# Two transformer blocks on one core: modulation by row products on VectorE in place of products and column sums on TensorE

## The chip, the core and the metric

The kernel runs on one core of one Trainium2 chip. Its metric is the device time of one execution in microseconds. Engines are named as the profile names them: PE is TensorE (PEld its weight loads), DVE is VectorE, ACT is ScalarE, POOL is GpSimd, SP is SyncE; a trailing q is the engine's own queue, from which it also issues DMAs. SBUF is the on-chip memory of 128 partitions, PSUM the accumulators that PE writes (banks `PB0` to `PB7`).

## The reference, cut to what matters

Two residual blocks over 256 tokens of width 1024, f32. Each block is modulated by a condition vector `c`: a vector-matrix product gives six vectors of 1024, which shift, scale and gate the two halves of the block.

```python
mod = jnp.einsum('bd,de->be', c, w_mod[l]) + b_mod[l]          # block 2: silu(c_2) @ w_ada_2 + b_ada_2
sh1, sc1, gt1, sh2, sc2, gt2 = jnp.split(mod, N_MOD, axis=-1)  # 6 x 1024
h = modulate(rmsnorm(x, norm1_g[l]), sh1, sc1)                 # norm * (1 + sc1) + sh1
z = jnp.einsum('bsd,de->bse', h, w_in[l])
...                                                            # pool mixer and attention, gated: y
x = x + gt1[:, None, :] * jnp.einsum('bsd,de->bse', y, w_out[l])
h2 = modulate(rmsnorm(x, norm2_g[l]), sh2, sc2)
x = x + gt2[:, None, :] * peer_ffn(h2, ...)                    # 16384 experts, rows of u and v
```

The weight matrix of the modulation is 1024 x 6144 f32 in each block, 24 MB. Block 2 has the same frame with other attention.

## The kernel before, in words

The kernel is five programs, one for each engine, ordered by semaphores that are written out by hand. Three of them share one long list of 651 weight tiles of 128 x 1024 f32 (512 KB). `SP` loads tile after tile into a ring of four slots. For each tile ACT rounds it to its high part (`WH`, line 1182, `fill` of the ACT program), DVE subtracts to get the low part (`WL`, line 1639, `fill` of the DVE program), and PE multiplies three products of high and low parts (lines 477 to 479, helper `three`). `WH` and `WL` hold three tiles (`NW`), so ACT may start tile t when PE has used tile t - 3 (`s_used`). `fill(k)` in a program means: see that tiles up to k + 2 are done; all other work of ACT and DVE stands between the `fill` calls, in program order.

Order of block 1: first norm and the modulation that it needs (chunks 0 to 7); pool input tiles, forget tile `W_F`; four Q steps and four K steps of two tiles each; the mixing loop `for i in range(10)`, two tiles a turn, which computes V and the output gates and beside them the attention of two heads a turn; then output projection, second norm, expert queries, the U phase (128 tiles of expert rows, activations), and the V phase (128 tiles, sums into four PSUM banks). Block 2 follows.

In a turn i of the mixing loop, PE runs `scores(i)` (lines 683, 686), `values(i - 2)` (711), one tile, `weights(i - 1)` (transposes, 698), one tile, and a step of the modulation. DVE runs `fill`, divides the exponentials of turn i - 1 by their sums (1819 to 1821), adds the mask to the scores of turn i and takes their maximum (1831, 1834), `fill`, copies of V (i < 4) and of y (i >= 2; line 1643), and, for i = 6 and 8, `mixed` for two parts of y (1805 to 1808); after i = 8 the diagonals for the broadcast of the gate (1729). ACT runs `fill`, the exponentials (1346), `fill`, copies of the turned weights (1186), sigmoids of the gates (1327; i = 5, 7, 9) and the modulation's step.

The modulation is cut into 48 chunks of 256 outputs, 24 a block, 1024 KB each. In block 1 (`mod_chunk`, line 544) PE multiplies the condition, padded to 32 columns, with a chunk, four partial sums on 32 partitions apart; ACT copies the result to `MR` (`chunk_out`), and `columns` (line 523) multiplies with ones, two one-column matmuls that put 2 x 128 outputs on partitions in `PB0`; DVE adds the bias (1649). Chunks 8 to 11 stand in the Q and K steps, 12 to 19 in turns 0 to 7, 20 to 23 after the output projection. `mod_step(g)` is the columns of the chunk before and the products of chunk g. ACT loads chunk g + 2 behind `chunk_out(g)` into two buffers. In block 2's modulation (chunks 24 to 47, in the V phase of block 1) DVE makes the partial sums instead (`chunk_step`: eight multiplications or multiply-adds by a value on each partition, 128 x 256, lines 2014 and 2017, two for each V tile); PE does the `columns` of chunks 24 to 35 in the V phase, and those of 36 to 47 (`LATE`) between the blocks, before `transposed(2)` (line 558), which waits for DVE's scaled rows (1646). The square of X at the start is DVE's line 1734.

## Time and profile before

| | us |
|---|---|
| median of 3 runs (2184.76 to 2185.3) | 2185.13 |
| the profiled execution: span from first to last instruction | 2183.5 |
| PE busy in it | 2135.9 |
| DVE busy | 1591.9 |
| ACT busy | 1297.9 |

The profile is that of one execution. In a timeline, a line is a run of equal instructions: start, us that they took, engine, line of the kernel, operation, output<-inputs, and in square brackets how long the engine had been idle before and what ended that. Matmuls overlap each other, so their distances are read between starts. In the groups the numbers after the bar are busy us, mean ns of one, and idle time before.

### The profile page before, as it was taken

How to read it: one execution, taken by the hardware profiler on the slowest of the kernel's cores; microseconds unless marked ns; L12 is line 12 of the kernel's file. 1: busy time of each engine (PE TensorE's matmuls, PEld its weight loads, DVE VectorE, ACT ScalarE, POOL GpSimd, SP SyncE). 2: the span in 40 equal slices, each digit the busy share in tenths (PEclk: the TensorE clock that was granted, in tenths of full speed). 3: DMA queues.
4: the chain of work that ended last, by engine and by line, in shares of the span. 5: the costliest groups of instructions: out<-in, count | busy, mean ns of one | idle time of the engine just before them, and what ended most of it. 6: DMA issues, size and time to landing. Idle time of an engine off the chain costs nothing.

```text
span 2183.5 us, 36554 instructions
## 1 busy us (share of the span) xinstructions
PE 2135.9 (98%) x13700; PEld 1904.0 (87%) x13700; DVE 1591.9 (73%) x3503; ACT 1297.9 (59%) x2442; POOL 100.4 (5%) x136
## 2 busy tenths in 40 slices
PE   7999999999999999999999998999999999999998
PEld 5988888888999988888889988888899998888886
DVE  3455659898888767888866655798988887555556
ACT  3355545666999754445545544565679986555554
POOL 0000000303000000000000000013030000000000
PEclk9999999999999999999989999999999999999999
DMA  8665566665444467778744634666654445566664
GB/s 334 203 210 180 178 184 185 200 185 183 136 127 127 155 202 284 282 276 289 257 145 135 204 97 129 187 189 194 192 172 127 126 127 174 182 194 193 194 194 133
DMA packets 110495, 407.42 MB, mean 187 GB/s; under 512 B 11504, under 2 KB 11888, under 8 KB 110064
## 3 DMA queue, kind: packets, MB, share of 16 engines
q1 hardware_dynamic: 98880, 361.81, 53.1%
q10 hardware_dynamic: 11440, 43.28, 5.1%
q8 instruction: 110, 1.80, 0.4%
q14 instruction: 65, 0.53, 0.1%
HBM read 403.99 MB, written 1.05 MB: 185 GB/s over the span
## 4 chain that ended last, share of the span: by engine, by line
PE 93%; DVE 3%; ACT 2%; issue 1%; POOL 1%; DMA 0%; ACTq 0%; DVEq 0%
PE PB L477 20%; PE PB L479 20%; PE PB L478 20%; PE PB L889 11%; PE PB L887 6%; PE PB L861 6%; PE PB L812 2%; PE PB L886 2%; PE PB L544 1%; PE PB L811 1%; PE PB L828 1%; PE PB L558 1%; PE PB L523 1%; POOL AR L2346 1%; DMA X<-in_x 0%
## 5 line engine op out<-in xcount | busy, mean ns | idle before, releaser
L1639 DVE TENSOR_TENSOR WL<-RING,WH 128x1024 fp32r<-128x1024 f32 x651 | 801.9, 1233 | 444.2 <-ACT WH L1182 442.1
L1182 ACT ACTIVATE WH<-RING 128x1024 fp32r<-128x1024 f32 x651 | 686.7, 1055 | 438.7 <-PE PB L479 430.9
L477 PE MATMUL PB<-WH,HX 128*128 128x512 f32 (+2 forms) x1344 | 494.4, 368 | 7.2 <-DVE HX L1694 3.3
L479 PE MATMUL PB<-WH,HX 128*128 128x512 f32 (+2 forms) x1344 | 490.5, 365 | 0.0
L478 PE MATMUL PB<-WL,HX 128*128 128x512 f32 (+2 forms) x1344 | 490.1, 365 | 0.0
L477 PE MATMUL PB<-HX,WH 128*128 128x256 f32 x1440 | 424.6, 295 | 6.8 <-DVE HX L1694 6.0
L479 PE MATMUL PB<-HX,WL 128*128 128x256 f32 x1440 | 409.4, 284 | 0.0
L478 PE MATMUL PB<-HX,WH 128*128 128x256 f32 x1440 | 409.1, 284 | 0.0
L889 PE MATMUL PB<-HX,WH 128*128 128x512 f32 x1092 | 389.1, 396 | 0.0
L887 PE MATMUL PB<-HX,WL 128*128 128x256 f32 x1248 | 322.4, 279 | 0.0
L477 PEld LDWEIGHTS PB<-WH,HX 128*128 128x128 f32 x1344 | 255.3, 190 | 51.4 <-issue 4.9
L479 PEld LDWEIGHTS PB<-WH,HX 128*128 128x128 f32 x1344 | 255.4, 190 | 40.4
L478 PEld LDWEIGHTS PB<-WL,HX 128*128 128x128 f32 x1344 | 255.5, 190 | 39.3
L477 PEld LDWEIGHTS PB<-HX,WH 128*128 128x128 f32 x1440 | 278.1, 193 | 13.2 <-issue 10.1
L478 PEld LDWEIGHTS PB<-HX,WH 128*128 128x128 f32 x1440 | 277.8, 193 | 0.3
L479 PEld LDWEIGHTS PB<-HX,WL 128*128 128x128 f32 x1440 | 277.1, 192 | 0.0
L887 PEld LDWEIGHTS PB<-HX,WL 128*128 128x128 f32 x1248 | 235.2, 188 | 13.5
L889 PEld LDWEIGHTS PB<-HX,WH 128*128 128x128 f32 x1092 | 204.9, 188 | 42.1
L1186 ACT ACTIVATE AR<-PB 128x256 f32<-128x256 f32 (+2 forms) x237 | 96.7, 415 | 220.3 <-PE PB L889 131.0
L1433 ACT ACTIVATE OH<-KC,GIT 128x128 f32<-128x128 f32 x512 | 162.4, 392 | 3.3 <-DVE GIT L1998 3.3
L2044 DVE TENSOR_SCALAR OH<-KC,GIT 128x128 f32<-128x128 f32 x512 | 142.3, 344 | 0.1
L861 PE MATMUL PB<-OH 128*128 128x128 f32 x1024 | 137.6, 277 | 1.9
(239 smaller groups left out, 2075.7 us busy)
## 6 DMA issues: line engine op xcount, KB each, us to landing
RING<-in_u SPq DMA_DIRECT2D x256, 512.0 KB, 3.7
RING<-in_v SPq DMA_DIRECT2D x256, 512.0 KB, 4.2
RING<-in_win SPq DMA_DIRECT2D x90, 512.0 KB, 3.9
AR<-in_wm ACTq DMA_DIRECT2D x40, 1024.0 KB, 6.5
RING<-in_wq SPq DMA_DIRECT2D x32, 512.0 KB, 3.7
AR<-in_wm SPq DMA_DIRECT2D x8, 1024.0 KB, 16.3
RING<-in_wout SPq DMA_DIRECT2D x16, 512.0 KB, 3.6
RING<-in_sk SPq DMA_DIRECT2D x8, 512.0 KB, 3.6
```

The lines of the kernel that those rows point to most:

```text
L477: e.matmul(o, ah, bh, start=start, stop=False)
L478: e.matmul(o, ah, bl, start=False, stop=False)
L479: return e.matmul(o, al, bh, start=False, stop=stop)
L812: r = e.matmul(PB[b][:, :], wh[:, k, :], HX[:, k, :], start=k == 0, stop=k == KT - 1)
L861: r = e.matmul(PB[b][:, 128 * t:128 * t + 128], OH[:, i, 0, t, :], OH[:, i, 1, t, :], start=True, stop=True)
L887: r = e.matmul(PB[b][:, 0:256], wl[:, m, :], HH[:, m, :], start=False, stop=False)
L889: r = e.matmul(PB[b][:, :], wh[:, m, :], HX[:, m, :], start=False, stop=m == KT - 1)
L1182: e.activation(hi(t), raw(("w", t), words(t)), ACT.Copy).then_inc(s_hi, 1)
L1186: e.activation(dst, src, ACT.Copy).then_inc(done, 1)
L1433: n = own.mark(e.activation(OH[:, i, 0, t, :], iota, ACT.Abs, scale=-1.0, bias=GIT[:, 1, 4 * q + t:4 * q + t + 1]))
L1639: e.tensor_tensor(lo(t), raw(("w", t), words(t)), hi(t).bitcast(F32), ALU.subtract).then_inc(s_lo, 1)
L2044: r = e.tensor_scalar(OH[:, i, 1, t, :], iota, GIT[:, 2, c:c + 1], GIT[:, 0, c:c + 1], ALU.is_equal, ALU.mult)
```

## The change

Chunks 8 to 19 of block 1 (the mixing gate and the second norm's shift and scale) and all 24 of block 2 are computed on DVE alone. Their weights are stored transposed, 128 outputs on partitions and the 1024 inputs along the row (`wr1`, `wr2`), and a chunk is two such halves. The condition is loaded as the same row on all partitions (`cr1`, `cr2`, 512 KB each, into the unused one-hot buffers `OH`). One `tensor_tensor_reduce` (`row_sum`) multiplies a half with the condition, in place, and writes its sum into the column of `MC` where the output belongs; the bias is added there (`add_rows`). PE and ACT have no part in these chunks but for their loads, which ACT issues (`rows_in`), into three buffers in block 1 and two in block 2, behind a wait for DVE's count `s_mr` or `s_mdv`. In the Q steps DVE makes 0, 1, 2, 2 row products, in each K step 2, in turn 0 of the mixing loop 2, and in turns 1 to 9 one. In the V phase it makes one behind every second tile. The Silu of block 2's condition moves from the start (8 columns) to the V phase (`n == 12`, 1024 columns). Chunks 0 to 7 and 20 to 23 stay as they are.

```diff
+MODS = [0, 4, 1, 5, 2, 6, 3, 7] + list(range(8, 24))
 N_START = 8
+N_ROWS = 12
+ROW_SLOT = {N_START + i: i % 3 if i < 11 else 0 for i in range(N_ROWS)}
+ROW_SLOT.update({24 + i: i % 2 for i in range(24)})
+ROW_LAND = {g: sum(ROW_SLOT[h] == s for h in ROW_SLOT if h <= g) for g, s in ROW_SLOT.items()}
...
-        PLACES = [ar(o, n, 2, 4, 256) for o, n in ((26112, 2), (1024, 4), (1024, 2))]
+        GATE2 = ar(1024, 4, 2, 4, 256)
+        ROWS1, ROWS2 = ar(26112, 3, 2, D), ar(1024, 2, 2, D)
         MR0 = ar(19232, N_START, 256)
-        LATE = 36
-        MRV = ar(8192, 48 - LATE, 256)
         COND = OH[:, 0, 0, 0:2, :].rearrange("p a (b n) -> p (a b) n", b=4)
+        CR = [OH[:, i, :, :, :].rearrange("p a t n -> p (a t n)") for i in (1, 0)]
...
+                    e.dma_start(CR[0], cr1).then_inc(s_cr, 16)
...
+                    e.wait_ge(s_gp, 64)
+                    e.dma_start(CR[1], cr2).then_inc(s_cr, 16)
...
-            def mod_step(g):
-                if g not in (N_START, 12):
-                    columns(g - 1)
-                mod_chunk(g)
...
-            mod_step(8)
...
-                    mod_step(9)
...
-            mod_step(10)
...
-                    mod_step(11)
...
-            columns(11)
...
-                if i < 8:
-                    mod_step(12 + i)
                 if i == 8:
-                    columns(19)
...
                     r.then_inc(s_used, 1)
-                    if blk == 0 and IN_V.get(n - 5, LATE) < LATE:
-                        columns(IN_V[n - 5])
...
-            for g in range(LATE, 48):
-                columns(g)
...
+            def rows_in(g, done=0):
+                if done:
+                    e.wait_ge(s_mr, done)
+                e.dma_start(row_chunk(g), row_source(g)).then_inc(chunk_landed(g)[0], 16)
...
-            e.activation(SM[:, C_C2:C_C2 + 8], SM[:, C_C2:C_C2 + 8], ACT.Silu).then_inc(s_silu, 1)
...
-                    chunk_in(8)
-                    chunk_in(9)
+                    for g in range(N_START, N_START + 3):
+                        rows_in(g)
...
+                if c == 3:
+                    rows_in(11, 1)
...
+                rows_in(12 + c, 2 + c)
...
+                if i < 3:
+                    rows_in(16 + i, 6 + i)
+                if i == 6:
+                    rows_in(19, 10)
...
+                    if blk == 0 and n == 12:
+                        e.wait_ge(s_cr, 32)
+                        e.activation(CR[1], CR[1], ACT.Silu).then_inc(s_silu, 1)
...
+            def add_rows(c0, c1, b_col, n):
+
+                e.tensor_tensor(MC[:, c0:c1], MC[:, c0:c1], SM[:, b_col:b_col + c1 - c0], ALU.add).then_inc(s_mod, n)
+
+            def row_sum(g, j):
+
+                w, c = row_chunk(g)[:, j, :], 2 * g + j
+                if j == 0:
+                    e.wait_ge(*chunk_landed(g))
+                if (g, j) == (N_START, 0):
+                    e.wait_ge(s_cr, 16)
+                if (g, j) == (24, 0):
+                    e.wait_ge(s_silu, 1)
+                r = e.tensor_tensor_reduce(w, w, CR[g // 24], 1.0, 0.0, ALU.mult, ALU.add, MC[:, c:c + 1])
+                if j:
+                    r.then_inc(s_mr if g < 24 else s_mdv, 1)
+
+            row_next = [0]
+
+            def row_sums(n):
+                for _ in range(n):
+                    row_sum(N_START + row_next[0] // 2, row_next[0] % 2)
+                    row_next[0] += 1
...
                 fill(k + 1)
+                row_sums((0, 1, 2, 2)[c])
...
                 fill(W_K + 2 * c + 1)
+                row_sums(2)
+                if c == 2:
+                    e.wait_ge(s_mr, 4)
+                    add_rows(16, 24, C_B1 + 16, 1)
...
-                if i == 0:
-                    e.wait_ge(s_mcol, 12)
-                    add_bias(0, C_B1, 16, 24)
+                row_sums(2 if i == 0 else 1)
...
-                    e.wait_ge(s_mcol, 20)
-                    add_bias(0, C_B1, 24, 40)
+                    e.wait_ge(s_mr, N_ROWS)
+                    add_rows(24, 40, C_B1 + 24, 1)
...
+            def chunk_step(n):
+
+                n0, t = n - (n - V_FIRST) % 4, (n - V_FIRST) % 4
+                if n0 in IN_V and t % 2:
+                    row_sum(IN_V[n0], t // 2)
...
-                        if IN_V.get(n - 7) == LATE - 1:
-                            e.wait_ge(s_mcol, LATE)
-                            add_bias(48, C_B2, 0, 24)
+                        chunk_step(n)
+                        if IN_V.get(n - 4) == 47:
+                            e.wait_ge(s_mdv, 24)
+                            add_rows(48, 96, C_B2, 2)
...
+    def rows(w):
+        n = w.shape[1] // 256
+        return w.reshape(1024, n, 2, 128).transpose(1, 3, 2, 0)
```

## Rows read from the trace of the kernel before

**Rows 1.** The page, part 1: busy us of each engine, share, instructions.

```profile
PE 2135.9 (98%) x13700; PEld 1904.0 (87%) x13700; DVE 1591.9 (73%) x3503; ACT 1297.9 (59%) x2442; POOL 100.4 (5%) x136
```

**Rows 2.** Groups by line and form: count, busy us, mean ns, idle before.

```profile
L544 PE MATMUL PB<-AR,OH 128*32 128x256 f32 x384 | 29.1, 431 | 9.6 <-DMA AR<-in_wm 9.4 <-DVE MC L1649 0.2
...
L523 PE MATMUL PB<-KC,MR 128*128 128x1 f32 x112 | 14.0, 229 | 0.0
...
L523 PE MATMUL PB<-KC,AR 128*128 128x1 f32 x80 | 11.1, 263 | 1.1 <-ACT AR L1186 1.1
```

**Rows 3.** Timeline of PE in the mixing loop: start us, us, engine, line, operation.

```profile
134.32 0.50 PE L523 MATMUL PB<-KC,MR 128*128 128x1 f32 x4
134.76 1.07 PE L544 MATMUL PB<-AR,OH 128*32 128x256 f32 x16
135.76 0.49 PE L683 MATMUL PB<-AR 64*128 64x128 f32 x4
...
141.04 0.82 PE L698 MATMUL PB<-KC,AR 128*128 128x128 f32 x6
...
144.56 0.50 PE L523 MATMUL PB<-KC,MR 128*128 128x1 f32 x4
```

**Rows 4.** The same, chunk 8.

```profile
55.78 1.94 PE L544 MATMUL PB<-AR,OH 128*32 128x256 f32 x16
```

**Rows 5.** Timeline of PE and of ACT where K ends.

```profile
116.68 0.50 PE L523 MATMUL PB<-KC,MR 128*128 128x1 f32 x4
117.58 0.49 PE L683 MATMUL PB<-AR 64*128 64x128 f32 x4 [0.40 <-issue]
...
116.88 0.60 ACT L1186 ACTIVATE AR<-PB 128x512 f32<-128x512 f32 x1 [1.76 <-PE PB L479]
```

**Rows 6.** Timeline of DVE at the start: the square of X.

```profile
11.46 1.23 DVE L1734 CUSTOM_DVE_ANT_0 AR<-X 128x1024 f32<-128x1024 f32 x1 [5.71 <-DMA X<-in_x]
12.61 0.08 DVE L1734 DVE_READ_ACCUMULATOR2_ANT ST<- 128x1 f32 x1
```

**Rows 7.** Timeline of DVE in two iterations of the mixing loop.

```profile
178.71 1.23 DVE L1639 TENSOR_TENSOR WL<-RING,WH 128x1024 fp32r<-128x1024 f32 x1 [2.81 <-ACT WH L1182]
...
180.91 0.35 DVE L1821 TENSOR_SCALAR AR<-AR 128x256 f32<-128x256 f32 x1
...
184.89 1.23 DVE L1639 TENSOR_TENSOR WL<-RING,WH 128x1024 fp32r<-128x1024 f32 x1 [2.08 <-ACT WH L1182]
...
186.37 0.42 DVE L1805 TENSOR_TENSOR AR<-AR 128x256 f32<-128x256 f32 x1
...
188.63 1.22 DVE L1639 TENSOR_TENSOR WL<-RING,WH 128x1024 fp32r<-128x1024 f32 x1
```

**Rows 8.** Timeline of ACT in the same stretch.

```profile
183.82 1.04 ACT L1182 ACTIVATE WH<-RING 128x1024 fp32r<-128x1024 f32 x1
```

**Rows 9.** Timeline of PE where the gate is broadcast.

```profile
205.02 0.50 PE L523 MATMUL PB<-KC,MR 128*128 128x1 f32 x4
206.43 0.35 PE L567 MATMUL PB<-AR,KC 128*128 128x128 f32 x1 [0.91 <-DVE AR L1729]
```

**Rows 10.** Timeline of PE in the V phase, around one column sum.

```profile
823.63 0.50 PE L523 MATMUL PB<-KC,MR 128*128 128x1 f32 x4
...
824.31 0.39 PE L478 MATMUL PB<-WL,HX 128*128 128x512 f32 x1
```

**Rows 11.** V phase, busy us (x instructions): PE, PEld, DVE, ACT, POOL; clock, DMA.

```profile
824.00:960.00 136.00, 136.00 (x623) 113.03 (x622) 109.57 (x188) 65.54 (x97) 0.00 (x0) 1.00 0.78 278
```

**Rows 12.** Timeline of PE between the blocks.

```profile
1101.67 5.62 PE L523 MATMUL PB<-KC,AR 128*128 128x1 f32 x48
1108.13 1.12 PE L558 MATMUL PB<-KC,AR 128*128 128x128 f32 x4 [0.84 <-DVE AR L1646]
```

**Rows 13.** The page, part 6: loads of the modulation weights, issue to landing.

```profile
AR<-in_wm ACTq DMA_DIRECT2D x40, 1024.0 KB, 6.5
...
AR<-in_wm SPq DMA_DIRECT2D x8, 1024.0 KB, 16.3
```

More of the change, by code:

```diff
@@ L49 @@
 N_TILES = 651
-MODS = [(0, m) for m in (0, 4, 1, 5, 2, 6, 3, 7)] + [(0, m) for m in range(8, 24)] + [(1, m) for m in range(24)]
+MODS = [0, 4, 1, 5, 2, 6, 3, 7] + list(range(8, 24))
 N_START = 8
+N_ROWS = 12
+ROW_SLOT = {N_START + i: i % 3 if i < 11 else 0 for i in range(N_ROWS)}
+ROW_SLOT.update({24 + i: i % 2 for i in range(24)})
+ROW_LAND = {g: sum(ROW_SLOT[h] == s for h in ROW_SLOT if h <= g) for g, s in ROW_SLOT.items()}
 V_FIRST = 22
@@ L401, in chunk, with row_chunk, nth @@
         def chunk(g):
-            if g < N_START:
-                return START[:, g, :, :, :]
-            return PLACES[0 if g < 20 else 1 if g < 24 else 2][:, g % 4 if 20 <= g < 24 else g % 2, :, :, :]
+            return START[:, g, :, :, :] if g < N_START else GATE2[:, g - 20, :, :, :]
+        def row_chunk(g):
+            return (ROWS1 if g < 24 else ROWS2)[:, ROW_SLOT[g], :, :]
+        def nth(g):
+            return g if g < N_START else g - N_ROWS
         def chunk_landed(g):
@@ L508, in columns @@
             def columns(g):
-                m = MODS[g][1]
+                m = MODS[g]
                 rows = chunk_sums(g)[2]
-                if g < 24:
-                    e.wait_ge(s_mev, g + 1)
-                else:
-                    e.wait_ge(s_mdv, g - 23)
-                if g in (24, LATE):
-                    e.wait_ge(s_mod, 7 if g == 24 else 8)
-                if g < N_START and g > 1:
-                    e.wait_ge(s_mod, g // 2)
-                if g in (20, 22):
-                    e.wait_ge(s_mod, 6)
+                e.wait_ge(s_mev, nth(g) + 1)
+                if g > 1:
+                    e.wait_ge(s_mod, min(g // 2, 4))
                 for j in range(2):
@@ L535, in mod_chunk @@
                 else:
-                    e.wait_ge(s_mev, g - 1 if 21 <= g < 24 else g)
+                    if g >= 22:
+                        e.wait_ge(s_mev, nth(g) - 1)
                     if g == 20:
                         e.wait_ge(s_up, 3)
-                    if g in (8, 12):
-                        e.wait_ge(s_mod, {8: 4, 12: 5}[g])
                 e.wait_ge(s_cond, 1)
@@ L1998, in chosen @@
                     e.tensor_copy(GIT[:, s, :], PB[4 + s][:, 0:256]).then_inc(s_git, 1)
-            chunk_sum = [0]
-            def chunk_step(n, half):
-                n0, t = n - (n - V_FIRST) % 4, 2 * ((n - V_FIRST) % 4) + half
-                if n0 not in IN_V:
-                    return
-                g = IN_V[n0]
-                w, rows, c = chunk(g)[:, t // 4, t % 4, :], chunk_sums(g)[2], SM[:, C_C2 + t:C_C2 + t + 1]
-                if t == 0:
-                    e.wait_ge(s_silu, 1)
-                    if g < LATE:
-                        e.wait_ge(s_mcol, g - 1)
-                    e.wait_ge(*chunk_landed(g))
-                    chunk_sum[0] = own.mark(e.tensor_scalar(rows, w, c, None, ALU.mult))
-                    return
-                own.done(chunk_sum[0])
-                r = e.scalar_tensor_tensor(out=rows, in0=w, scalar=c, in1=rows, op0=ALU.mult, op1=ALU.add)
-                if t < 7:
-                    chunk_sum[0] = own.mark(r)
-                else:
-                    r.then_inc(s_mdv, 1)
+            def chunk_step(n):
+                n0, t = n - (n - V_FIRST) % 4, (n - V_FIRST) % 4
+                if n0 in IN_V and t % 2:
+                    row_sum(IN_V[n0], t // 2)
             def peer(blk, n_q, n_u, n_v, gate):
@@ L2326, in peer @@
                             e.wait_ge(s_rope, 6)
+                        else:
+                            e.wait_ge(s_mr, 9)
                         for i in range(16):
@@ L2449 @@
         "u1": experts(i["peer_u"]), "v1": i["peer_v"][0],
-        "wm2": halves(i["w_ada_2"][0]),
+        "wr2": rows(i["w_ada_2"][0]),
         "win2": np.concatenate([tiles(w2[:, :1024]), halves(w2[:, 1024:1536]), tiles(w2[:, 1536:3072]),
```

67 lines of the change are left out of this document (27 added, 40 removed).

## The prediction, made before the changed kernel ran

> **What bounds the kernel now.** I read the page's busy table first, then the groups of instructions, then the timeline of each engine. TensorE (PE) is busy 98% of the span [rows 1]; what shortens the kernel is PE time, and what lengthens it is PE waiting. The modulation costs PE two kinds of work [rows 2]: 384 weight-vector products (16 records for each of 24 chunks) and 192 one-column sums (4 records for each of 48 chunks). The change takes away 12 chunks of the first and 36 of the second. "Busy" overstates them, because matmuls are pipelined; I take distances between starts. In the mixing loop the columns of a chunk take 134.76 - 134.32 = 0.44 us and the products of a chunk 135.76 - 134.76 = 1.00 us [rows 3].
>
> **Part 1, ahead of the mixing loop (chunks 8 to 11).** Four products and four column sums leave PE. Chunk 8 runs at half clock, 1.94 us busy [rows 4] against 1.07 at full clock [rows 3]; the projections that move into this place run at half clock too, so I count it at its full-clock 1.00. Chunks 9, 10, 11: 3.00. Columns 8, 9, 10: 3 x 0.44 = 1.32. Columns 11: nothing. PE starts them at 116.68 and its next work, the first scores, at 117.58, 0.90 later, of which 0.44 is the columns; the scores wait for ScalarE's copy of kT, which runs from 116.88 to about 117.5 whatever PE does [rows 5]. Sum: 5.3 us.
>
> What is put in their place is 13 row products on VectorE (DVE) up to the end of K's four steps, two a step at most. One row product multiplies 128x1024 f32 with 128x1024 f32 and sums it. The nearest row is the square of X at the start, the same instruction with the same sizes: 1.23 us, and its accumulator is read 12.61 - 11.46 = 1.15 after its start [rows 6]. I take 1.17 a product. Two of them are 2.3 us of DVE in front of the next weight tile's subtraction. A tile is let go by PE three tiles ahead of its use, so two tiles of about 2.9 us (3.52 between 141.04 and 144.56 with six transposes in it [rows 3]) lie between; ScalarE takes 1.04 and DVE 1.23 of them [rows 7, 8], which leaves 3.5 us. The products fit, so I cost them at nothing here; this cover is thin in the K step that also scales yaT (3.4 us in the same queue), hence up to 3 us lost at the upper end.
>
> **Part 2, the mixing loop (chunks 12 to 19).** Eight products and eight column sums leave PE: 8 x 1.00 + 8 x 0.44 = 11.5 us. Here I don't believe the whole of it, because a second loop runs beside PE's. An iteration of PE lasts 144.56 - 134.32 = 10.24 us [rows 3], and without the chunk 8.80. The other loop goes DVE low part of a tile, DVE softmax, ScalarE exponentials (in order ahead of its next tile), DVE low part of the second tile, DVE copy of y. From one start, 178.71, to the end of that copy, 186.37, it is 7.66 us [rows 7]; the second tile comes from ScalarE at 183.82, which in its program stands behind the exponentials of this same turn, and DVE sits idle 2.08 us for it [rows 7, 8]. With a row product behind it the loop is 7.66 + 1.17 = 8.83, and 9.16 in iterations 2 and 3, which copy v too (one more copy of 0.33). So the two loops are now equally long, and DVE loses the time in which it used to stand idle.
>
> How far may DVE lag? PE's transposes of the second head come, after the change, 141.04 - 134.32 - 1.44 + 0.28 = 5.56 us behind the boundary of an iteration; DVE has that head ready 180.91 + 0.35 - 178.71 = 2.55 after the low part starts. A lag of more than about 2.95 us stalls PE. I walk through it, lag of the low part's start and then the stall. Iteration 1: 2.45 (two products in iteration 0, no values yet, limit 2.1), 0.3. Iteration 2: 2.95, 0. 3: 3.3, 0.4. 4: 3.3, 0.4. 5: 3.0, 0. 6: 3.3 (ScalarE's sigmoids with a table load come first), 0.4. 7: iteration 6 has `mixed` twice, 188.63 - 186.37 = 2.26 us [rows 7], which was hidden in DVE's idle time: lag 5.3, stall 2.4. Iteration 8 has no scores, so PE comes 1.5 earlier to the transposes and found DVE late already; the chunk's 1.44 taken from it is worth 0.1. Its end is the broadcast of the gate, for which DVE must do copy, row product and `mixed` twice first: PE waited there already (1.41 us from the columns at 205.02 to the broadcast at 206.43, [rows 9]), and by my walk the row product comes on top of that path; these two places give back 2.3. Given back in all: 0.3 + 0.4 + 0.4 + 0.4 + 2.4 + 2.3 = 6.2. Kept: 11.5 - 6.2 = 5.3, say 5.4 because PE had small waits of its own before. The two ends: 0 (every chunk's place taken by a DVE wait) and 11.5.
>
> **Part 3, the V phase of block 1.** Twelve column sums leave PE (chunks 24 to 35). A matmul of this phase follows the one before at 0.23; from the columns' start 823.63 to the second matmul behind them 824.31 it is 0.68 [rows 10], so one column sum costs 0.68 - 0.23 = 0.45 with the pipeline's restart: 12 x 0.45 = 5.4 us, all on the path, as PE is busy 136.00 us of 136.00 there and DVE 109.57 [rows 11]. DVE's eight multiply-adds of a chunk become two row products, 2.3 us in 11.4. One of them lies behind every second tile, less than the 3.5 us of cover. ScalarE gets a `Silu` over the 1024 columns of the second condition with its table load, about 2.4 us once (a 1024-wide tile takes it 1.04 [rows 8]); it has 65.54 busy of 136 [rows 11], so nothing. SyncE's queue gets one more 512 KB load behind the one of `final_g`, whose waits it shares; its extra wait (all gates multiplied) is met before the phase starts. Nothing.
>
> **Part 4, between the blocks.** The last 12 column sums, 48 records, stand at 1101.67; PE then waits for the scaled rows of DVE and starts transposing at 1108.13, "idle before <-DVE L1646" [rows 12]. They fill a wait that DVE's chain sets, and removing them brings nothing. DVE's add of the bias that waited for them goes too (under 0.2 us, behind the broadcast). At the start, ScalarE's Silu goes from a time in which it waits for X, and the first condition's 512 KB load lies behind weights that are used late: nothing.
>
> **Transfers.** Chunks are 1024 KB each as before, and are issued by ScalarE, which now waits for DVE's count in front of an issue; tiles and softmax are queued behind that wait. In my walk the count is there one step before each issue. The three-buffer ring starts with three loads instead of two.
>
> **Sum.** 5.3 + 5.4 + 5.4 = 16.1 us. The profiled span is 2183.5, so the changed one would be 2167.4; the median of the runs, 2185.13, lies 1.6 above that span, so 2169.0 us. The clock adds noise: the stretch at half clock at 55.78 costs 0.9 us in that chunk alone [rows 3, 4], and such stretches can move when the work moves; I allow 2 us either way.
>
> **Rivals.**
> (a) PE keeps everything. If ScalarE's and DVE's loop is shorter than I think, or my lag limits are too strict, it is 5.3 + 0.4 + 11.5 + 5.4 = 22.6: 2162.5 us. For it: DVE is idle 2.08 us in such an iteration [rows 7]. Against it: that idle time is a wait for ScalarE inside the loop, not a reserve. Chance 0.20.
> (b) DVE also delays the Q and K steps. Two products ahead of a tile, the yaT scaling behind them, and chunks that land late: a loss of up to 3 us there, and as much again in the loop if its lag starts larger. Saved about 10: 2175 us. Chance 0.13.
> (c) A row product costs twice my price, 2.3 us. Then a turn of the loop is 7.66 + 2.3 = 10.0. The walk gives turns of 10.5, 9.9, 10.2, 10.2, 9.9, 9.9, 12.3 and 13.1 to the broadcast, 86.0; before it is 81.5 (72.1 from 134.32 to 206.43, and 9.4 for the first turn, a full one without column sums and values [rows 3, 9]). So the loop loses 4.5 us instead of gaining 5.4; Q and K keep 1.5; the V phase keeps 5.4 (two tiles are 5.5 us, DVE would need 5.3). Saved 2.4: 2182.7 us, no difference. For it: the measured instruction reads the same X twice. Against it: the subtraction of the low part reads two different arrays of SBUF and takes 1.23 as well [rows 7]. Chance 0.05.
> The Trainium skill has a rule by which (c) would happen: its page "Vector Engine (DVE) Microarchitecture Reference", section 7, "Points that are easy to get wrong", says that the scalar-tensor-tensor form with two SBUF sources wider than bf16 runs at half throughput, since no port is left to read the accumulator. By that rule the kernel would end at 2182.7, by the row at 2169.0. The square of X, two f32 sources from SBUF with an accumulator, was not halved.
> (d) Slower: late landings. DVE now waits in order for a chunk, with tiles behind it. In K a chunk is issued at the end of a step and its first product comes 5.8 us later. The median landing is 6.5 us [rows 13], so DVE waits 0.7, inside the cover. Beyond 5.8 + 3 = 9 us each further us is PE's, for each of chunks 12 to 16; from 9 + 16.1 / 5 = 12.2 us on the change is a loss. The chunks at the start, beside everything else, took 16.3 [rows 13]. At 13.5 us: 5 x 4.5 - 16.1 = 6.4 slower, 2191.5. Against it: transfers are thinner in K. Chance 0.04.
> (e) The change does less than it says: the column sums of chunks 20 to 23 and their products stay on PE, as written, and are in no term of mine. No chance of its own.
>
> **How the numbers follow.** Forecast 0.58, 2166 to 2172 by itself. The range reaches over (a) and (b) with the clock: 2161 to 2176; (c), (d) and tails are outside. This kernel's runs tell 0.2%, about 4.4 us, from no change. Faster by more than that: 0.58 + 0.20 + 0.13 = 0.91. Within: 0.05 (c). Slower: 0.04 (d).
>
> **What would show it.** The row product at 1.2 us with a start-to-start of 1.17; if 2.3, (c). Distance from the first matmul of the mixing loop's iterations: 8.8 to 9.2 us, and 11 for iteration 7; if 8.8 throughout, (a). PE waits on DVE's softmax scaling (line 1821) in front of the transposes, and longer than 0.91 us on DVE's diagonal (line 1729) in front of the broadcast. V phase: 5.4 shorter, no gap every fourth tile. Between the blocks: an idle PE of about 6.5 us where the columns were, and the same distance from PE's last V matmul to the transposes. DVE waiting for a DMA in K for more than 3 us would be (d).

## The result, and the profile after

The changed kernel takes 2170.91 us (median of 5 runs, 2169.6 to 2172.1) against 2184.76 us before (5 runs on the same chip): ratio 0.9939, 95% interval 0.9929 to 0.995, or 13.3 us saved, 11 to 15.5 by the interval. The forecast was 2169.0, so the total came within 2 us. Its parts did not: the gain forecast for one was 6.6 us too high, and the others and the clock made it up.

The page of the kernel after, whose span is 2168.7 us against 2183.5: busy time of each engine [rows 1], and its loads of modulation weights with the median time from issue to landing [rows 13].

```profile
PE 2106.7 (97%) x13364; PEld 1881.0 (87%) x13364; DVE 1599.7 (74%) x3454; ACT 1295.9 (60%) x2430; POOL 100.4 (5%) x136
...
AR<-in_wr ACTq DMA_DIRECT2D x36, 1024.0 KB, 7.3
...
AR<-in_wm SPq DMA_DIRECT2D x8, 1024.0 KB, 16.1
```

PE is busy 29.2 us less, and the span is 14.8 us shorter. "Busy" overstated the removed work, as the forecast said. DVE's total barely moves: what row products bring in block 1 leaves in block 2's chunk steps.

The row product, L1652, all 72 of them, with duration min/median/max in ns, first and last start in us:

```profile
L1652 DVE CUSTOM_DVE_ANT_0 AR<-AR,OH x72: 1212/1219/1227, 66.8 to 1072.5; 128x1024 f32<-128x1024 f32 x72
```

It costs 1.22 us, as the square of X did (1.23) [rows 6].

The table sets distances between starts in PE's timeline beside each other, for both kernels and all experiments (from one profiled execution each; medians and ratios are of the timed runs, the ratio to runs of the kernel before on the same chip, whose medians lay between 2183.28 and 2185.09). "First scores" is the first matmul of the mixing loop. "Scores 1 to 7" is from the second group of scores to the eighth and last, six turns. "To tile" is from that last group to the first weight tile behind the gate's broadcast. "Last phase" is from there to the transposes between the blocks.

| kernel | median us | ratio to before, 95% | first scores | scores 1 to 7 | to tile | last phase |
|---|---|---|---|---|---|---|
| before | 2184.76 | | 117.58 | 60.60 | 23.53 | 897.68 |
| after | 2170.91 | 0.9939, 0.9929 to 0.995 | 110.10 | 56.40 | 30.23 | 891.49 |
| r_early | 2168.81 | 0.9924, 0.9911 to 0.9938 | 109.70 | 54.24 | 31.21 | 891.66 |
| r_slot | 2168.29 | 0.9925, 0.9912 to 0.9939 | 110.24 | 53.23 | 29.75 | 891.65 |
| r_skip | 2168.47 | 0.9928, 0.9914 to 0.9941 | 109.57 | 54.64 | 25.32 | 891.55 |
| r_mix | 2166.1 | 0.9919, 0.9906 to 0.9933 | 109.04 | 54.85 | 24.06 | 891.56 |
| r_short1 | 2166.37 | 0.9917, 0.9903 to 0.993 | 110.02 | 52.62 | 25.17 | 891.52 |
| r_best | 2161.9 | 0.9897, 0.9882 to 0.9913 | 109.14 | 52.64 | 22.58 | 891.66 |
| best_short | 2161.14 | 0.9893, 0.9877 to 0.991 | 109.62 | 52.61 | 22.57 | 891.62 |
| d_slot | 2166.86 | 0.9923, 0.9909 to 0.9937 | 109.31 | 54.39 | 26.42 | 891.42 |
| d_behind | 2177.31 | 0.9969, 0.9956 to 0.9981 | 111.61 | 60.70 | 30.67 | 892.23 |
| r_shortV | 2171.75 | 0.9941, 0.9926 to 0.9957 | 110.30 | 55.09 | 31.22 | 891.70 |
| b_nocol | 2177.67 | 0.997, 0.9959 to 0.9982 | 114.71 | 60.59 | 23.53 | 891.79 |
| b_mix | 2181.29 | 0.9994, 0.9985 to 1.0004 | 114.92 | 60.59 | 22.30 | 898.50 |

Read the first two rows. Before the loop the kernel after is 7.5 us ahead. From the first scores to the tile behind the broadcast it takes 204.17 - 110.10 = 94.07 us where the kernel before takes 92.87. Eight chunks' products and column sums are gone from this stretch, and it became 1.2 us longer. In the last phase it gains 6.2. What is behind that (between the blocks and block 2) is 2.3 us shorter.

**Where the loop loses it.** What PE waited for from its first scores to the tile behind the broadcast, in the kernel after (total us, times, longest):

```profile
PE PB L570 <- DVE AR L1741: 3.3, 3, 3.0
PE PB L706 <- DVE AR L1631: 3.0, 4, 1.9
PE PB L693 <- DVE AR L1838: 2.3, 3, 1.2
...
PE PB L493 <- DVE AR L1631: 0.6, 1, 0.6
```

And the same view of the kernel before:

```profile
PE PB L567 <- DVE AR L1729: 1.4, 4, 0.9
...
PE PB L544 <- DVE MC L1649: 0.2, 1, 0.2
```

1.6 us of waits for DVE have become 9.2 (3.3 + 3.0 + 2.3 + 0.6). They stand for the diagonals of the broadcast (L570), the `values` matmuls, which wait for DVE's copy of the last turn's y (L706 on L1631), and the transposes behind the softmax scaling (L693 on L1838); the 0.6 stands at the first weight tile of turn 1. Three kinds of place can be seen in the timelines. First, PE's turns, by their scores:

```profile
117.55 0.49 PE L678 MATMUL PB<-AR 64*128 64x128 f32 x4
...
127.85 0.49 PE L678 MATMUL PB<-AR 64*128 64x128 f32 x4
...
173.95 0.49 PE L678 MATMUL PB<-AR 64*128 64x128 f32 x4
```

The first full turn, 117.55 to 127.85, takes 10.30 us; the next ones take 8.90, 9.54, 9.13, 8.90 and 9.63 to the last group at 173.95. DVE where K ends shows why the first is long:

```profile
108.82 1.22 DVE L1652 CUSTOM_DVE_ANT_0 AR<-AR,OH 128x1024 f32<-128x1024 f32 x1
...
112.14 1.23 DVE L1652 CUSTOM_DVE_ANT_0 AR<-AR,OH 128x1024 f32<-128x1024 f32 x1 [2.09 <-DMA AR<-in_wr]
```

The second product of K's last step waits 2.09 us for its chunk to land, and the tile's low half and the first softmax stand behind it. Second, DVE in a turn of the loop, here the one with two mixings:

```profile
171.93 0.17 DVE L1851 TENSOR_SCALAR AR<-AR 128x2 f32<-128x2 f32 x1
174.18 1.23 DVE L1627 TENSOR_TENSOR WL<-RING,WH 128x1024 fp32r<-128x1024 f32 x1 [2.08 <-ACT WH L1170]
175.32 0.42 DVE L1631 COPY AR<-PB 128x256 f32<-128x256 f32 x1
175.66 1.22 DVE L1652 CUSTOM_DVE_ANT_0 AR<-AR,OH 128x1024 f32<-128x1024 f32 x1
...
176.80 0.42 DVE L1822 TENSOR_TENSOR AR<-AR 128x256 f32<-128x256 f32 x1
...
179.06 1.22 DVE L1627 TENSOR_TENSOR WL<-RING,WH 128x1024 fp32r<-128x1024 f32 x1
```

DVE is idle 2.08 us ahead of the low half at 174.18, waiting for ScalarE. Only behind that come the copy of y, the row product (175.66) and the mixing (176.80 on), so that the next low half starts at 179.06. In the kernel before, the same chain ran from 184.89 to 188.63, 3.74 us [rows 7]; here it is 4.88. Third, PE in the two turns that follow:

```profile
180.99 1.21 PE L693 MATMUL PB<-KC,AR 128*128 128x128 f32 x6 [1.16 <-DVE AR L1838]
...
186.93 1.33 PE L706 MATMUL PB<-AR 128*64 128x256 f32 x8 [1.87 <-DVE AR L1631]
...
198.87 0.68 PE L570 MATMUL PB<-AR,KC 128*128 128x128 f32 x4 [2.98 <-DVE AR L1741]
```

It waits 1.16 us in turn 7, 1.87 at the start of turn 8 and 2.98 behind it. And behind the last two of these waits the granted clock is down. The windows hold busy us (and records) of PE, PEld, DVE, ACT and POOL, then the clock:

```profile
183.00:187.00 4.00, 2.13 (x20) 1.96 (x20) 1.92 (x4) 3.98 (x10) 0.00 (x0) 1.00 0.04 17
187.00:191.00 4.00, 4.00 (x22) 3.50 (x23) 2.57 (x6) 2.27 (x4) 0.00 (x0) 0.57 0.45 135
191.00:200.00 9.00, 5.87 (x48) 5.50 (x47) 6.62 (x18) 1.82 (x3) 0.00 (x0) 1.00 0.85 295
200.00:205.00 5.00, 4.85 (x26) 3.48 (x26) 1.70 (x5) 2.14 (x3) 0.00 (x0) 0.66 0.25 99
```

Over 183 to 187 PE is busy 2.13 of 4 us, over 191 to 200 it is busy 5.87 of 9; in the stretches behind, the granted clock is 0.57 and 0.66 of 2.4 GHz, that is at 1.2 GHz most of the time. The weight tile from 188.19 to 192.22 takes 4.03 us, the one from 181.95 to 185.06 took 3.11; `values` ahead of it takes 1.26 (188.19 - 186.93), where they took 176.69 - 175.88 = 0.81 a turn earlier, the broadcast 204.17 - 198.87 = 5.30 instead of 4.02 (from 206.43 [rows 9] to the tile at 210.45 in the kernel before). The clock adds some 2.6 us (0.9 + 0.4 + 1.3) to the waits. In the kernel before it stays full in the whole loop. That the waits brought it down is not shown; what the experiments say of it stands with r_slot and r_mix.

### The profile page after: what moved, and what is told of

Its sections match the earlier page's. It is cut to its first block, busy times and chain, and to the rows that moved or that the text cites. A ratio compares the mean times of both kernels' runs of the same rounds, so it can differ in the third digit from the quotient of the medians.

```text
span 2168.7 us, 35775 instructions
## 1 busy us (share of the span) xinstructions
PE 2106.7 (97%) x13364; PEld 1881.0 (87%) x13364; DVE 1599.7 (74%) x3454; ACT 1295.9 (60%) x2430; POOL 100.4 (5%) x136
## 4 chain that ended last, share of the span: by engine, by line
PE 89%; DVE 6%; ACT 3%; issue 1%; DMA 1%; POOL 1%; ACTq 0%; DVEq 0%
PE PB L493 20%; PE PB L494 19%; PE PB L495 19%; PE PB L881 11%; PE PB L879 6%; PE PB L853 6%; PE PB L804 2%; PE PB L878 2%; DVE WL L1627 1%; ACT WH L1170 1%; PE PB L803 1%; PE PB L820 1%; ACT AR L1329 1%; POOL AR L2341 1%; PE PB L561 1%
## 6 DMA issues: line engine op xcount, KB each, us to landing
AR<-in_wm SPq DMA_DIRECT2D x8, 1024.0 KB, 16.1
```

## The experiments

Theory A, formed from these traces: the row product costs because of its place in DVE's queue (behind the copy of y, in front of the mixing and of the broadcast's diagonals) and because of a chunk that is issued late; the time that it takes is free elsewhere. Theory B: the amount of DVE's work, or the traffic of chunks and products, costs wherever it stands. All edits are to the kernel after unless it is said otherwise. The ratios are known to about 0.0014, or 3 us, so a single move that gains 2 to 5 us is not clear of the kernel after by its time alone and is read from its trace; by time, r_best, best_short and d_behind are clear of it.

**r_early: the loads of the K steps issued earlier.**

```diff
                 fill(k)
+                rows_in(12 + c, 2 + c)
                 fill(k + 1)
...
-                rows_in(12 + c, 2 + c)
```

> Kernel after, with one thing moved: in the K steps ScalarE issues the load of the next modulation chunk between its two weight tiles, and no longer behind the copy of kT, so 5 to 8 us earlier. Theory A (the last K step waited for a chunk that was issued late: issued 103.65, product started 112.14 where VectorE was free at 110.05, and 0.9 us once before that): VectorE's wait for DMA in the K steps, 2.9 us, goes; the first scores' maxima come 2 us earlier and the first turn of the mixing loop falls from 10.30 to about 8.4 us; 2 us less, about 2169 us. Rival (the chunk lands when the queues let it, whenever it is issued, or the first turn waits for something else): the product still starts at 112, and the time stays at 2171 us.

2168.81 us. DVE where K ends:

```profile
108.43 1.22 DVE L1652 CUSTOM_DVE_ANT_0 AR<-AR,OH 128x1024 f32<-128x1024 f32 x1
...
109.58 1.22 DVE L1652 CUSTOM_DVE_ANT_0 AR<-AR,OH 128x1024 f32<-128x1024 f32 x1
```

No product waits for a chunk: the two follow each other, the low half starts at 110.72 instead of 113.29, and the first full turn is 8.14 us instead of 10.30. The other turns are unchanged (8.90, 9.54, 9.13, 8.90, 9.63), so the late chunk touches the first alone. The 2.16 us is partly that execution's luck: with issues as in the kernel after, this product waited 0.32 us for its chunk in r_skip, 0.52 in r_slot, 0.75 in r_shortV, 1.33 in d_behind and 1.52 in d_slot, and the first full turns were 8.54, 8.73, 8.98, 9.54 and 9.73: that wait plus 8.2 us each time, as in the kernel after (2.09 and 10.30). The fault is real but varies by about 2 us from one execution to another.

**r_slot: the row product in DVE's idle time.**

```diff
                         e.tensor_scalar(SX[:, 2, si, :], ...).then_inc(s_nm, 1)
+                if 1 <= i < 8:
+                    row_sums(1)
                 fill(n + 1)
...
-                row_sums(2 if i == 0 else 1)
+                if not 1 <= i < 8:
+                    row_sums(2 if i == 0 else 1)
```

> Kernel after, with one thing moved: in turns 1 to 7 of the mixing loop VectorE takes its row product right behind the negated maximum, ahead of the second weight tile's low half, and no longer behind the copy of y. The same work is done in all. In the kernel after VectorE stands idle there for 2.08 us in each turn (172.10 to 174.18), waiting for ScalarE, and the product needs 1.3 us. Theory A (the order costs, since the product behind the y copy lengthens the chain from one turn's values to the next turn's exponentials): turns 1 to 6 fall from 8.9 to 9.6 us to about 8.8 to 8.9, 2.1 us in all, turn 7 loses the product's 1.2 us, and the two half-clock stretches at 187.2 and 200.8 go or shrink, worth up to 3.4 us: 5 to 7 us less, 2164 to 2166 us. Theory B (it is the amount of VectorE's work, or the traffic of the chunks and products, wherever they stand): within 1 us of the kernel after, 2170 to 2172 us.

2168.29 us. All turns from the second to the sixth are 8.90 us, as expected, so the place was what they paid for. But the total is 2.6 us down and not 5 to 7. PE's waits in the loop:

```profile
PE PB L570 <- DVE AR L1741: 3.0, 1, 3.0
PE PB L706 <- DVE AR L1631: 1.9, 1, 1.9
```

The waits for the softmax scaling are gone; those for `values` at the start of turn 8 (1.9) and for the broadcast (3.0) are as long as before. The half-clock stretches grew from 3.4 and 3.4 us to 3.4 and 6.8: the tile behind `values` takes 4.48 us (183.41 to 187.89) and the broadcast 6.12 (194.54 to 200.66), so the 3.4 us that the clock was expected to give back did not come. In turn 8 the product still stands where it stood, ahead of the mixing and the diagonals. PE's wait for `values`, then DVE's product of turn 8:

```profile
182.44 0.87 PE L706 MATMUL PB<-AR 128*64 128x256 f32 x8 [1.86 <-DVE AR L1631]
```

```profile
190.71 1.22 DVE L1652 CUSTOM_DVE_ANT_0 AR<-AR,OH 128x1024 f32<-128x1024 f32 x1
```

So this run doesn't tell what the broadcast waits for. `values` starts 11.52 us behind the last scores (170.92 to 182.44) where it was 12.98 (173.95 to 186.93): the product did hold it up, but ahead of the transposes. The length of the wait itself is set behind them. From the softmax scaling on, DVE needs 5.9 us to the end of its copy of y (180.93 to 186.79 in the kernel after), and PE has only transposes and one tile to do meanwhile.

**r_skip: no row product in turns 6, 7 and 8.**

```diff
-                row_sums(2 if i == 0 else 1)
+                row_sums((2, 1, 1, 1, 1, 1, 0, 0, 0, 2)[i])
...
             fill(W_GATE + 12)
+            row_sums(1)
             fill(W_GATE + 13)
+            row_sums(1)
```

> Kernel after, with the row products of turns 6, 7 and 8 of the mixing loop (those with the mixing of y in them, and the one right ahead of the gate's broadcast) put off: two stand in turn 9, one behind each of the next two weight tiles, and the bias is added behind them. The same work is done in all. Theory A (the loss is made in turns 6 to 8, where the product stands beside the mixing, 2.4 us, and ahead of the broadcast): turn 7 falls from 13.0 or so (173.95 to 186.93) by 1.3 us, turn 8 by up to 1.3, the broadcast starts another 1.3 us earlier, and with shorter stalls the half-clock stretches at 187.2 and 200.8 (3.4 us of time each, 1.7 lost) shrink: 4 to 6 us less, 2165 to 2167 us. Rival (the first five turns cost as much, by 8.9 to 9.6 against 8.8): only 1 to 2 us less, 2169 to 2170 us. By theory B (the amount counts): within 1 us of the kernel after.

2168.47 us, less gain than expected, in runs that spread from 2165.45 to 2171.47; its profiled execution, with a span of 2163.6, is the fastest of them:

```profile
PE PB L706 <- DVE AR L1631: 3.0, 4, 1.9
PE PB L570 <- DVE AR L1741: 1.5, 4, 1.1
```

The broadcast's wait fell from 3.0 to 1.1 us, so the product of turn 8 was part of it; the longest for `values` is still 1.9. From the last scores to the tile it is 25.32 instead of 30.23, and there is no half-clock stretch in the loop. Of this, 2 us come back in block 2, where the half-clock stretches are longer (1075.1 us from the transposes between the blocks to the end against 1073.0).

**r_mix: the mixing moved, the row products left where they are.**

```diff
-                row_sums(2 if i == 0 else 1)
-                if i in (6, 8):
-                    mixed(i - 6)
-                    mixed(i - 5)
                 if i == 8:
                     e.wait_ge(s_mod, 5)
                     bcast(0, MC[:, 16:24])
+                row_sums(2 if i == 0 else 1)
+                if i in (6, 7):
+                    mixed(i - 6)
+                if i == 8:
+                    mixed(2)
+                    mixed(3)
```

> Kernel after with only the mixing of y moved, row products as they are: one mixing in turn 6 in place of two, the second in turn 7, and in turn 8 the diagonals of the broadcast ahead of the row product and both mixings. Theory A: the broadcast starts as soon as the weight tile before it ends (in the kernel after 195.90, where it started at 198.87): 3.0 us; turn 7 is 1.25 us shorter, since only one mixing (1.25 us) stands ahead of its softmax scaling, and the second fits in VectorE's wait of 1.4 us at 187.92 to 189.31; the half-clock stretches of the loop (two of 3.4 us) go or shrink, up to 3.4 us. 4 to 7 us less than the kernel after, 2164 to 2167 us. Rival (the mixing is not what is waited for in turn 7, but the copies of pT behind the exponentials): only the 3 us of the broadcast, 2168 us.

2166.1 us, in the expected range. The broadcast begins in PE's timeline without a wait, and the clock over the same turns is full:

```profile
191.46 0.61 PE L570 MATMUL PB<-AR,KC 128*128 128x128 f32 x4
```

```profile
183.00:196.00 13.00, 11.88 (x91) 10.14 (x92) 10.10 (x28) 6.31 (x10) 0.00 (x0) 1.00 0.70 242
```

"To tile" falls from 30.23 to 24.06 us, the most of any single move. The wait of 1.9 for `values` at the start of turn 8 remains even here, with its half-clock stretch gone:

```profile
183.21 0.87 PE L706 MATMUL PB<-AR 128*64 128x256 f32 x8 [1.87 <-DVE AR L1631]
```

So that wait alone doesn't decide on the clock. Behind 1.86 or 1.87 us of it a half-clock stretch follows in the kernel after, r_early, r_slot and r_shortV, and none in r_skip, r_mix and r_short1, nor behind 2.10 in d_slot. The longer wait can't be the cause of the first stretch either: in the kernel after the stretch begins at 187.2 and that wait at 195.9. What decides is open.

**b_mix: the same move in the kernel before.**

> Kernel before (no row products) with the mixing of y on VectorE moved as in r_mix: one in turn 6 and one in turn 7 in place of two in turn 6, and in turn 8 the diagonals of the broadcast ahead of both mixings. In the kernel before TensorE stands still there only from 205.53 to 206.43 and the turns are 10.23 us of its own work. If the stalls are new, made by TensorE's shorter turns and the row products: about 1 us less than the kernel before, 2183 to 2184.5 us, against 4 to 7 us for the same move in the kernel after. If this order had cost as much all along: 2178 to 2181 us.

2181.29 us, 0.9994 of the kernel before, 0.9985 to 1.0004: 1.3 us by the ratio and 2.0 by the medians, no difference that can be told. It came out below the range expected, by 1.7 us. In its trace the broadcast follows the column sums:

```profile
202.16 0.50 PE L523 MATMUL PB<-KC,MR 128*128 128x1 f32 x4
202.52 0.69 PE L567 MATMUL PB<-AR,KC 128*128 128x128 f32 x4
```

The distance is 0.36 us where it was 1.41 [rows 9], and "to tile" goes from 23.53 to 22.30. The same order of DVE's work that cost 1.2 us before the change costs 30.23 - 24.06 = 6.2 after it, the clock's 2.6 included. The change made an old order expensive.

**r_short1: the work itself taken away.**

```diff
+                q = 8 if g < 24 else 1024
-                r = e.tensor_tensor_reduce(w, w, CR[g // 24], ...)
+                r = e.tensor_tensor_reduce(w[:, 0:q], w[:, 0:q], CR[g // 24][:, 0:q], ...)
```

> Kernel after, with block 1's row products taken over the first 8 of 1024 elements; waits, loads and order stay, most of the sum is left out. It prices VectorE's work in block 1 as a whole. If that work is what kept the gain of the PE work that was removed: first turns near 8.4 us, all others at the 8.8 us that the PE work needs, the half-clock stretches in the loop gone: 8 to 10 us less than the kernel after, 2161 to 2163 us. If the loads of the chunks (their landing and their queue) are what costs: the same waits stay, and the time is within 2 us of the kernel after, 2169 to 2171 us.

Most of each sum is left out. 2166.37 us, 3 us above what was expected. Turns are 8.12 and 8.90 us. In the loop:

```profile
PE PB L706 <- DVE AR L1631: 1.9, 1, 1.9
PE PB L570 <- DVE AR L1742: 1.6, 4, 1.1
```

Without the products' time 1.9 us for `values` and 1.1 for the broadcast remain. The 1.1 belongs to the two mixings, which stand between the copy of y and the diagonals. The 1.9 is theirs only in part: in r_best, with one mixing in turn 6 and no product there, 1.3 is left. And the loop as a whole, 195.26 - 110.02 = 85.24 us, is only 7.6 shorter than before, not 11.5.

**d_slot and d_behind: the product of turns 1 to 7 made twice**, in the idle time (on r_slot) and behind the copy of y (on the kernel after).

```diff
+                if 15 <= 2 * (g - N_START) + j <= 21:
+                    own.done(own.mark(e.tensor_tensor_reduce(w, w, CR[g // 24], ...)))
```

> Kernel r_slot (row product ahead of the second weight tile's low half), with the product of turns 1 to 7 made twice, 1.3 us more of VectorE's work in each of seven turns; seven sums of the second norm's modulation come out other than they should. VectorE has 2.08 us free there, two products take 2.6. Theory A (place): the low half starts 0.5 us later, which is still 0.5 us or more ahead of where TensorE wants that tile; turns 1 to 6 stay at 8.90 us, turn 7 and the broadcast, where the mixing follows, lose 0.5 each: 0 to 1.5 us over r_slot, 2168 to 2170 us. Theory B (amount): 9.1 us of VectorE's work more, and as much as in the run with the product doubled behind the copy of y.

> Kernel after (row product behind the copy of y), with the product of turns 1 to 7 made twice; seven sums of the second norm's modulation come out other than they should. Theory A (place): VectorE's chain from the copy of y to the next softmax scaling is already what TensorE waits for in turns 2 and 3 (9.54 and 9.13 against 8.90) and in 6 and 7, so most of the 1.3 us is added in each turn: turns of 9.9 to 10.2, 6 to 9 us over the kernel after, 2177 to 2180 us. Theory B: the same rise as with the product doubled in the other place.

The second pass multiplies its row again and so changes seven sums. 2166.86 against r_slot's 2168.29: ratios 0.9923 and 0.9925, no price that can be told for 9 us of DVE's work more. d_slot's loop also kept the full clock where r_slot's did not. 2177.31 against 2170.91: ratios 0.9969 and 0.9939, 6.5 us for the same work in the other place. PE's waits, first d_slot, then d_behind:

```profile
PE PB L570 <- DVE AR L1743: 2.7, 4, 2.2
PE PB L706 <- DVE AR L1631: 2.4, 2, 2.1
PE PB L693 <- DVE AR L1840: 1.1, 2, 0.9
```

```profile
PE PB L693 <- DVE AR L1840: 4.9, 8, 2.4
PE PB L706 <- DVE AR L1631: 3.0, 6, 0.7
```

Behind the first full turn, turns are 8.90 us (one 9.06) in d_slot and 10.05 to 10.39 in d_behind, which waits 8 times for the softmax scaling. This is the clearest run against theory B.

The Trainium skill has a rule that fits: its page "Perfetto Trace Analysis", section "Per-engine timelines", has ScalarE, VectorE and GpSimd as strict first-in first-out, TensorE with limited reordering. These two runs agree, at 0 and 6.5 us for equal work.

**r_shortV: block 2's products cut short, in the last phase of block 1.**

> Kernel after, with block 2's row products taken over the first 8 of 1024 elements, so most of their sums is left out; waits, loads and order stay. 48 products of 1.22 us, 57 us of VectorE's time in block 1's last phase, go. If they are hidden there, as the forecast has it: no change, 2169.5 to 2172 us. If they hold up the weight tiles' low halves or the X copies of that phase at all: up to 5 us less.

The edit is that of r_short1 with the condition turned round, `g >= 24`. 2171.75 us, ratio 0.9941 against 0.9939; the last phase is 891.70 us against 891.49. They are hidden, all 57 us of them.

**b_nocol: the kernel before without block 2's column sums.**

```diff
             def columns(g):
 
+                if g >= 24:
+                    return
```

> Kernel before, with the column sums of block 2's 24 chunks left out on TensorE (12 in block 1's last phase, 12 between the blocks), so block 2's modulation is not computed; VectorE's chunk steps stay. If these matmuls alone make the gain there: 5.4 to 6 us in the last phase of block 1 (12 steps of 0.45 to 0.5), nothing for the 12 between the blocks, which fill a wait, up to 1.7 us by a shorter half-clock stretch (13.7 us in the kernel before, 10.2 after): 2177.5 to 2179.5 us. If the gain of that phase came from VectorE's shorter chunk steps instead: within 1 us of the kernel before, 2184 to 2186 us.

DVE's waits for the counts of these sums are lowered to match. 2177.67 us, ratio 0.997 (0.9959 to 0.9982), 6.5 us. The last phase is 5.9 us shorter than before, with DVE's chunk steps in place, so the matmuls alone are the gain. Between the blocks, where the 48 records are gone, PE waits instead:

```profile
1092.67 0.39 PE L479 MATMUL PB<-WH,HX 128*128 128x512 f32 x1
1099.36 0.90 PE L560 MATMUL PB<-KC,AR 128*128 128x128 f32 x3 [6.31 <-DVE AR L1648]
```

From the last weight matmul to the transposes it is 6.69 us, and 1108.13 - 1101.44 = 6.69 in the kernel before, too.

**r_best: the three moves together** (r_early, r_slot, r_mix).

> Kernel after with three things moved and the same work done: the row product of turns 1 to 7 ahead of the second weight tile's low half, the chunk loads of the K steps issued between ScalarE's two weight tiles, and on VectorE in turn 6 one mixing of y in place of two, the second in turn 7, and in turn 8 the diagonals of the broadcast ahead of the row product and of both mixings. The single runs so far show the parts: turns of 8.90 us with the product moved (that is what TensorE's own work needs there), a first turn of 8.14 with the early loads. Theory A (order, not amount): scores at 109.7, 117.2, 125.3 and then 8.90 apart to 169.8, turn 7 about 10, the broadcast from about 189 to 193 us where the kernel after has 198.87 to 204.17, no half-clock stretch in the loop: 11 us ahead there, of which block 2's gaps give back up to 2 by longer half-clock stretches (as without the products: 8.9 ahead at 204, 6.9 at the end). 2160 to 2162.5 us. Theory B (the gains do not add, or the freed time returns in the next wait): no better than the best single move, 2166 to 2168 us.

2161.9 us: ratio 0.9897 (0.9882 to 0.9913) to before, 9 us better than the kernel after, with the same work. All turns are 8.90, the first 8.14, and the broadcast starts at 187.87. PE's waits in the loop, and DVE behind the negated maximum (L1851):

```profile
PE PB L706 <- DVE AR L1631: 1.3, 1, 1.3
...
PE PB L570 <- DVE AR L1741: 0.5, 3, 0.2
PE PB L693 <- DVE AR L1838: 0.2, 1, 0.2
```

```profile
166.88 0.17 DVE L1851 TENSOR_SCALAR AR<-AR 128x2 f32<-128x2 f32 x1
166.96 1.22 DVE L1652 CUSTOM_DVE_ANT_0 AR<-AR,OH 128x1024 f32<-128x1024 f32 x1
...
169.13 1.23 DVE L1627 TENSOR_TENSOR WL<-RING,WH 128x1024 fp32r<-128x1024 f32 x1 [0.95 <-ACT WH L1170]
```

The product runs from 166.96 in what was a wait; 0.95 us of that wait is left ahead of the low half at 169.13.

**best_short: r_best with block 1's products cut short.**

> Kernel r_best (2161.9 us) with block 1's row products taken over the first 8 of 1024 elements, most of their sums left out: 29 us of VectorE's work gone, 24 products of 1.2 us. In the kernel after the same cut brought 4.5 us (2170.9 to 2166.4). Theory A (in r_best every product stands where VectorE is idle): nothing is left to gain, turns stay at 8.14 and 8.90 us, 2161 to 2163 us. Theory B (part of the price is the work itself, wherever it stands): 1.5 to 4 us less, 2158 to 2160 us.

2161.14 us, ratio 0.9893 against 0.9897: nothing left to gain. The cut that brought 4.5 us in the kernel after brings 0.8 here, within the spread.

## Why the prediction was right, and where it was wrong

**Part 1, ahead of the loop: right, 0.7 us low.** Forecast 5.3. d_behind has the code of the kernel after up to the first scores and half-clock stretches within 0.3 us of the same places as the profiled execution of before: 117.58 - 111.61 = 6.0. r_mix and b_mix, which share another pattern of them, give 114.92 - 109.04 = 5.9. So 1.5 us of the 7.5 between the two profiled executions belongs to the execution, not to the change: b_mix and b_nocol run the code of before up to there and are 2.7 and 2.9 us earlier than it. Row products next to Q and K cost PE nothing.

**Part 2, the mixing loop: the mechanism right, the term mis-sized.** Forecast +5.4, measured -1.2, 6.6 us too high. The walk had turns 3 and 4 stalled by 0.4 each, turn 5 by nothing, turn 6 by 0.4: measured 0.64, 0.23, 0 and 0.73 over 8.90. What it had wrong, term by term:
- The nominal 11.5 us, eight chunks of 1.44. In r_best, where PE waits for DVE for 2.0 us against 1.6 before, the loop takes 191.81 - 109.14 = 82.67 us, 10.2 less than before. A turn falls by 10.23 - 8.90 = 1.33, not by the 1.44 that lie between the starts of what was taken out; why 0.11 a turn stays is not shown. 1.3 us.
- The first turn, 0.3 forecast, 10.30 - 8.14 = 2.16 measured. I had costed landings in the loop at nothing and put them in rivals (b) and (d); the last chunk of K took 8.5 us from its issue at 103.65 to the product at 112.14. 1.9 us.
- Turns 2 to 6: 1.2 forecast, 1.6 measured. 0.4 us.
- Turns 7 and 8 with the broadcast: 2.4 + 2.3 forecast. Measured, 30.23 against 22.58 in r_best: 7.65. 2.9 us. Of these 2.6 is the clock, which was down behind PE's new waits; I allowed 2 us for stretches that move, and none for new ones behind the stalls that I forecast.

One link of the chain was missing from the walk: `values` waits for DVE's copy of the turn before, so the limit for DVE's lag is not that of the transposes alone (0.58 us in turn 3, 1.87 at turn 8). Another was in it and misread: in turn 8 the diagonals stand behind row product and both mixings although they need neither. The forecast took that for a price of the row product. r_mix shows it as a matter of order, 3.0 us that no product has to cost.

**Part 3, the last phase: right.** 5.4 forecast, 5.9 by b_nocol for the same twelve column sums (0.49 each, not 0.45), 6.2 between the profiles. The window answering to [rows 11]:

```profile
824.00:960.00 136.00, 136.00 (x602) 112.61 (x601) 106.69 (x151) 69.66 (x101) 0.00 (x0) 1.00 0.83 281
```

PE is busy all the time with 602 records in place of 623, DVE with 106.69 us in place of 109.57.

**Part 4, between the blocks: right.** Zero forecast, an idle PE of about 6.5 us in the columns' place:

```profile
1089.00 0.39 PE L495 MATMUL PB<-WH,HX 128*128 128x512 f32 x1
1095.66 1.54 PE L561 MATMUL PB<-KC,AR 128*128 128x128 f32 x6 [6.28 <-DVE AR L1634]
```

6.28 us idle, and 1095.66 - 1089.00 = 6.66 from the last weight matmul, as long as before.

**The rest.** 2.3 us between the blocks and in block 2 were in no term. The work there is the same; the kernel after has 13.7 us of half-clock stretches around and behind the transposes and the kernel before 20.5 (both leave out the last one, in which the program ends). Here the clock gave about what it took in the loop. Over all traces the time of this part follows these stretches: 1073.0 to 1073.1 us in after, r_early, r_slot and r_shortV with 13.7 us; 1074.7 to 1075.4 in eight kernels and 1073.7 in b_mix with 20.5; 1076.0 in r_mix with 23.9. The four with 13.7 are the ones whose clock also fell in the loop, but d_behind, whose clock fell there too, has 20.5. So no rule comes out of it, and why the two go together the runs don't tell.

**The rivals.** (a), PE keeps everything, 2162.5: not this kernel, but r_best's 2161.9. DVE's 2.08 us were a reserve after all, once the product was put inside them; "a wait for ScalarE inside the loop, not a reserve" holds for the place that the change chose. (b) is half true: nothing lost for PE in Q and K, 1.9 in the loop's first turn. (c) fell with 1.219 us for the product. The Trainium skill's page "Vector Engine (DVE) Microarchitecture Reference", section 7, has its scalar-tensor-tensor form halved for two SBUF sources that are not bf16; this multiply-and-sum over two different f32 arrays takes as long as the square of one array and as the subtraction, 1.22 us, so the rule doesn't carry over to it. (d): the median landing was 7.3 us and DVE waited 2.9 us in K, short of the 3 named as its sign.

The total was right partly because the loop's 6.6 us were offset: 0.7 more in part 1, 0.8 in part 3, 1.5 of the execution at the start and 2.3 behind. That makes 14.8 us between the spans where 16.1 were forecast.

## What to carry to other kernels

Work that is moved to a second engine is priced by its place in that engine's queue: look for the stretch in which that engine waits for something else, put the work there, and check what stands behind it. When the bounding engine's turn gets shorter, walk every wait it makes on the other engine again, the old ones included: an order that cost 1.2 us before the change cost 6.2 behind it, and changing it was worth as much as the work itself. Compare early stretches of two profiles only between executions whose clock fell at the same places.

## What was not expected of the hardware

New stalls of 1.87 and 2.98 us on PE were followed by stretches at 1.2 GHz that added 2.6 us; with the longer wait removed (r_mix, r_best) the clock stayed full over the whole loop, although waits of 1.9 and 1.3 us remained. d_slot, with waits of 2.1 and 2.2 us there, kept the full clock as well, and r_slot lost it behind a wait of 1.86 us. One and the same load took 8.5 us to land in one execution and kept DVE waiting 2.09 us; in others of the same issue order DVE waited 0.3 to 1.5 us.
